# A mixture-of-experts layer: bias through the matrix product, one clamp, all weight slots split, the second product by column halves

## What is computed

```python
logits = (xt @ w_router) + b_router;  top_vals, top_idx = lax.top_k(logits, 4);  gates = softmax(top_vals)
# for each expert e and the tokens routed to it:
h = xblk @ w1[e] + b1[e]                      # 1024 x 2048
x_glu = minimum(h[..., ::2], 7);  x_lin = clip(h[..., 1::2], -7, 7)
a = x_glu * sigmoid(1.702 * x_glu) * (x_lin + 1)
out[token] += gate * (a @ w2[e] + b2[e])      # w2: 1024 x 1024
```

## Time and profile before

| | us |
|---|---|
| median of three runs | 2392.95 |
| the profiled execution | 2390.75 |
| its span, first to last instruction | 2389.0 |
| TensorE busy | 2191.3 (92%) |
| VectorE busy | 1499.4 (63%) |
| ScalarE busy | 972.6 (41%) |
| mean granted TensorE clock | 0.955 |

### The profile page before, as it was taken

How to read it: one execution, slowest core, us unless ns; L and a number is a source line. 1 busy time by engine, 2 the same in 40 slices (tenths; PEclk the granted TensorE clock), 3 DMA queues, 4 the chain that set the end, 5 groups by cost and what they waited for, 6 DMA issues and landing times.

```text
span 2389.0 us, 30180 instructions
## 1 busy us (share of the span) xinstructions
PE 2191.3 (92%) x9492; PEld 1592.8 (67%) x9493; DVE 1499.4 (63%) x2207; ACT 972.6 (41%) x1146; POOL 283.6 (12%) x245
## 2 busy tenths in 40 slices
PE   6999687997789999999899999999899999999997
PEld 4454277544468876686686868686667886886885
DVE  4013566233677676767777667777777677677765
ACT  3023444011344444444444444444444444444443
POOL 1000300001101111111011111111012012011111
PEclk9999799898799999999999999999999999999998
DMA  7000200200697669869978786868989668668666
GB/s 244 0 1 4 94 1 1 88 27 31 231 367 275 227 243 357 314 224 331 354 269 294 245 318 220 306 221 315 336 317 338 215 238 309 228 217 304 232 216 231
DMA packets 244997, 524.29 MB, mean 219 GB/s; under 512 B 17575, under 2 KB 22759, under 8 KB 240736
## 3 DMA queue, kind: packets, MB, share of 16 engines
q1 hardware_dynamic: 220990, 467.84, 54.8%
q0 software_dynamic: 23904, 55.95, 6.3%
q10 hardware_dynamic: 66, 0.02, 0.0%
HBM read 522.20 MB, written 32.11 MB: 232 GB/s over the span
## 4 chain that ended last, share of the span: by engine, by line
PE 76%; issue 4%; DVE 1%; DVEq 1%; ACT 1%; POOL 0%; POOLq 0%; ACTq 0%
PE ps L1028 19%; PE ps L1030 19%; PE ps L1029 19%; PE ps L1080 8%; PE ps L953 5%; PE ps L1063 2%; PE ps L1022 1%; PE ps L972 1%; PE ps L1015 1%; PE ps L985 1%; PE ps L965 0%; PE ps L934 0%; ACT uT L666 0%; DVE xT_lo L1469 0%; PE ps L907 0%
## 5 line engine op out<-in xcount | busy, mean ns | idle before, releaser
L1469 DVE TENSOR_TENSOR w_lo<-ring,w_hi 128x2048 fp32r<-128x2048 f32 x330 | 755.0, 2288 | 261.5 <-ACT w_hi L710 261.1
L710 ACT ACTIVATE w_hi<-ring 128x2048 fp32r<-128x2048 f32 x327 | 625.1, 1916 | 452.9 <-PE ps L1030 421.8
L1028 PE MATMUL ps<-w_hi,xT_hi 128*128 128x512 f32 x1212 | 499.5, 412 | 11.6 <-DVE xT_lo L1469 10.2
L1030 PE MATMUL ps<-w_hi,xT_lo 128*128 128x512 f32 x1212 | 474.9, 392 | 0.0
L1029 PE MATMUL ps<-w_lo,xT_hi 128*128 128x512 f32 x1212 | 473.3, 391 | 0.0
L1028 PE MATMUL ps<-w_hi,actT_hi 128*128 128x512 f32 x720 | 303.8, 422 | 73.7 <-issue 73.7
L1029 PE MATMUL ps<-w_lo,actT_hi 128*128 128x512 f32 x720 | 294.7, 409 | 0.0
L1030 PE MATMUL ps<-w_hi,actT_lo 128*128 128x512 f32 x720 | 294.0, 408 | 0.0
L1028 PEld LDWEIGHTS ps<-w_hi,xT_hi 128*128 128x128 f32 x1212 | 228.2, 188 | 76.4 <-issue 18.0
L1029 PEld LDWEIGHTS ps<-w_lo,xT_hi 128*128 128x128 f32 x1212 | 228.5, 188 | 53.2 <-issue 9.1
L1030 PEld LDWEIGHTS ps<-w_hi,xT_lo 128*128 128x128 f32 x1212 | 228.0, 188 | 50.2
(11 more groups left out here) (260 smaller groups left out, 2087.4 us busy)
## 6 DMA issues: line engine op xcount, KB each, us to landing
ring<-in_w SPq DMA_DIRECT2D x390, 1024.0 KB
b1b<-in_b SPq DMA_DIRECT2D x33, 1024.0 KB, 11.7
xh<-in_x SPq DMA_DIRECT2D x2, 2048.0 KB, 17.7
work<-in_w_out SPq DMA_DIRECT2D x1, 4096.0 KB, 12.7
token_rows<-uT POOLq DMA_DIRECT2D x8, 512.0 KB, 2.9
out<-xh SPq DMA_DIRECT2D x8, 512.0 KB, 2.6
work<-in_w_in SPq DMA_DIRECT2D x2, 1536.0 KB, 19.4
uT<-in_w_mem_kv SPq DMA_DIRECT2D x1, 2048.0 KB, 17.8
```

The costliest lines, as they stand in the source:

```text
L710: act_e.activation(w_hi[s % SPLIT][:, :, :], slot(s), ACT.Copy).then_inc(hi_ready, counted(s, whole))
L1028: pe.matmul(acc, hi, whi, start=first, stop=False)
L1030: return pe.matmul(acc, lo, whi, start=False, stop=last)
L1469: return dve.tensor_tensor(lo, x, hi.bitcast(F32), ALU.subtract)
```

## The change

- `add_bias` goes. The biases of all experts are put into SBUF once before the loop, as a high and a low part with 1 added in the odd columns (`b1w`). `select_expert` makes a 64 x 128 selection matrix for the pass on VectorE, and every odd slot begins with one matmul of it by 512 columns of `b1w`, for each group.
- VectorE then takes one minimum against a pair of limits, from PSUM (`clamp`); the lower clamp goes into `times_gelu`.
- ScalarE does `gelu(j)` ahead of `split_hi(2j+5)`, where it did it behind.
- No slot is left whole: single passes split all twelve.
- A slot of w2 now holds 256 rows by all 1,024 columns; `down(s, b)` computes one column half. Double passes run the halves b=0 of slots 8 and 9 and then the halves b=1. In single passes the results stand in banks 1 and 4 and the next tokens in 5 and 6, so the wait of slot 9 for `xlo_ready` is left to double passes; there it stands before `down(8, 1)`.
- `combine` moves from VectorE to ScalarE, as a copy out of PSUM times the gate, at the end of its list. The scatter adds into the output; the gather of the output rows is dropped. The 1 MB bias load of each pass is dropped.

```diff
+        def y_bank(groups, g, b):
+            return 4 * b + g if len(groups) == 2 else 1 + 3 * b
...
                     for g in groups:
-                        po.indirect_dma_start(out=rows[:, g, :], out_offset=None, in_=out[0],
...
                         po.wait_ge(combined[g], before[g] * 2 + 4)
+                        po.indirect_dma_start(out=out[0], out_offset=by_index(idx_cur, g), in_=y[:, g, :],
+                                              in_offset=None, bounds_check=last_row, oob_is_err=False,
+                                              compute_op=ALU.add).then_inc(scattered[g], 16)
...
+                    def combine(b):
+                        if b == 0:
+                            act_e.wait_ge(idxcur_ready, p + 1)
+                            act_e.wait_ge(gate_copied, p + 1)
+                            act_e.wait_ge(y_half, p + 1)
+                        else:
+                            act_e.wait_ge(w_used, p12 + (SPLIT + 12))
+                        for g in groups:
+                            act_e.activation(y[:, g, b * HALF:(b + 1) * HALF], ps[:, y_bank(groups, g, b), :], ACT.Copy,
+                                             scale=gate_cur[:, g:g + 1]).then_inc(combined[g], 1)
...
                     for j in range(4):
+                        gelu(j)
                         split_hi(2*j+5)
-                        gelu(j)
...
                     split_hi(13)
                     split_hi(14)
+                    combine(0)
+                    combine(1)
...
                         acc = ps[:, 2 * (j % 2) + g, :]
+                        if kh == 1:
+                            if j == 0:
+                                pe.wait_ge(b1_lo, 1)
+                                pe.wait_ge(sel_ready, p + 1)
+                            pe.matmul(acc, sel[:, :], b1w[:, j * HALF:(j + 1) * HALF], start=False, stop=False)
...
-                            if s in whole:
-                                m = pe.matmul(acc, xT_f[:, k, :], slot(s)[:, k, :], start=kk == 0, stop=kk == KD - 1)
...
+                    def down(s, b):
+                        j = s - 8
+                        if b == 0:
+                            wait_words(s)
                         for g in groups:
+                            if b == 0:
+                                pe.wait_ge(alo_ready[g], pieces[g] + (j + 1))
...
+                            for k in range(2):
+                                m = three(ps[:, y_bank(groups, g, b), :], actT_hi[g][:, 2 * j + k, :],
...
+                    down(8, 0)
+                    if len(groups) == 2:
+                        down(9, 0)
+                        transpose_act(2)
+                        pe.wait_ge(xlo_ready[0], p + 2)
+                        down(8, 1)
+                        down(9, 1)
+                    else:
+                        down(8, 1)
+                        transpose_act(2)
+                        down(9, 0)
+                        down(9, 1)
                     transpose_act(3)
+                    for s in (10, 11):
+                        down(s, 0)
+                        down(s, 1)
...
+                    def clamp(j):
+
+                        dve.wait_ge(w_used, used + (2 * j + 2))
                         for g in groups:
...
+                            dve.tensor_tensor(hm[:, g, j % 2, :], ps[:, 2 * (j % 2) + g, :],
+                                              limit[:, :, :].rearrange("p n two -> p (n two)"), ALU.min).then_inc(h_free[g], 1)
...
+                    select_expert()
                     split_lo(3)
...
+                    take_gates()
                     split_lo(4)
                     for j in range(4):
-                        add_bias(j)
+                        clamp(j)
...
-                        split_lo(2 * j + 5)
+                        if j < 3:
+                            split_lo(2 * j + 5)
+                        times_gelu(j)
                         if j == 3:
...
+                            split_lo(11)
                         if j:
                             take_alo(j - 1)
                         split_lo(2 * j + 6)
...
                     take_alo(3)
+                    if len(groups) == 1:
+                        take_xlo(p + 2, 0, next_x_bank(groups))
                     split_lo(13)
-                    combine(0)
                     split_lo(14)
-                    combine(1)
```

More of the change, by code:

```diff
@@ L178, in hymba_layer @@
         gatesT, b2_sb = uT[:, 11, :], uT[:, 12, :]
+        b1_raw = uT[0:2 * E, 0:2, :].rearrange("p a b -> p (a b)")
         early.close()
@@ L192, in hymba_layer @@
         actT_hi, actT_lo = ([sb(f"{n}{g}", [P, KD, P], F32R) for g in range(2)] for n in ("actT_hi", "actT_lo"))
[L193 to L196, removed]
+        sel = sb("sel", [2 * E, P], F32R)
+        hm = sb("hm", [P, 2, 2, HALF])
+        gel, act = (sb(n, [P, 2, 2, HALF // 2]) for n in ("gel", "act"))
+        y = sb("y", [P, 2, D])
         ps = ctx.enter_context(nc.psum_tensor("ps", [P, 8, HALF], F32))
@@ L275, in hymba_layer, with next_x_bank, ids_bank @@
             ptac.append(ptac[-1] + (heads(kind) // 2 + 1) // 2)
[L277 to L283, removed]
+        def next_x_bank(groups):
+            return 5 if len(groups) == 1 else 4
+        def ids_bank(groups):
+            return 3 if len(groups) == 1 else 6
+        def y_bank(groups, g, b):
+            return 4 * b + g if len(groups) == 2 else 1 + 3 * b
         def slot(s):
@@ L354, in _ @@
             sp.dma_start(b2_sb[0:E, :], b2[0]).then_inc(b2_in, 16)
+            for half in range(2):
+                sp.dma_start(b1_raw[half * E:(half + 1) * E, :], b1[0]).then_inc(b1_in, 16)
             sp.wait_ge(ttab_ready, 1)
@@ L1084, in up @@
[L1084 to L1104 removed]
+                            m = three(acc, xT_hi[g][:, kk, :], xT_lo[g][:, kk, :],
+                                      w_hi[s % SPLIT][:, k, :], w_lo[s % SPLIT][:, k, :], kk == 0, kk == KD - 1)
@@ L1483, in _ @@
             make_onehot(0)
-            make_idx(1)
+            make_idx(1, 6)
             make_onehot(1)
+            dve.wait_ge(b1_in, 32)
+            odd = b1_raw.rearrange("p (n two) -> p two n", two=2)[:, 1, :]
+            dve.tensor_scalar(odd, odd, 1.0, None, ALU.add).then_inc(b1_plus, 1)
             for u in range(2 * NT):
@@ L1556, in take_alo, with select_expert @@
                                      actT_hi[g][:, 2 * j:2 * j + 2, :]).then_inc(alo_ready[g], 1)
-                    def combine(b):
-                        dve.wait_ge(w_used, used + (11 + b))
-                        for g in groups:
-                            if b == 0:
-                                dve.wait_ge(rows_in[g], rows16[g])
-                            rb = rows[:, g, b * HALF:(b + 1) * HALF]
-                            dve.scalar_tensor_tensor(out=rb, in0=ps[:, 4 * b + g, :], scalar=gate_cur[:, g:g + 1], in1=rb,
-                                                     op0=ALU.mult, op1=ALU.add).then_inc(combined[g], 1)
+                    def select_expert():
+                        dve.tensor_tensor(sel[:, :], ident[0:2 * E, bass.ds(e, 1)].to_broadcast([2 * E, P]),
+                                          ident[0:2 * E, bass.ds(e + E, 1)].to_broadcast([2 * E, P]), ALU.add).then_inc(sel_ready, 1)
@@ L1579, in body @@
                         if j == 3:
-                            take_xlo(p + 2, 0)
-                        times_gelu(j)
+                            if len(groups) == 2:
+                                take_xlo(p + 2, 0, next_x_bank(groups))
+                            split_lo(11)
                         if j:
```

194 lines of the change are left out of this document (71 added, 123 removed).

## The result

The changed kernel takes 2552.4 us (2549.8 to 2553.4, four runs) against 2394.2 for the kernel before, measured beside it on the same chip: a ratio of 1.068 [1.066, 1.070]. It is slower, as forecast, but by 158 us instead of 87, and outside the range of the prediction. The profiled execution has a span of 2551.7 us.

The account below looks back on a forecast made before the run. VectorE's list with forced waits was taken to bound single passes after the change, TensorE double ones. 2390.75 + 57 (single) + 29 (double) + 1 (bias preparation) = 2478 us, slower; range 2440 to 2540 us.

Parts of the forecast that it names:

- Clamp to split_lo: VectorE in single passes: from clamp(j) it must wait for ScalarE's gelu, then split_hi; 3.0 us, four times, 12.0 us.
- TensorE's longest stop: Single passes: TensorE stands 4.9 us before activation transposes 3, waiting for take_alo(2), with 0.42 us matmul steps behind.
- the sign that was to speak for the scatter: If VectorE's longest stop came before the index step, the scatter would be the cause; no size given.
- It gets eight bias matmuls: 1.8 us: Double passes: TensorE stays the bound and pays 1.8 us for eight added bias matmuls.
- 0.4 us more of stop at the head: Head of double passes: TensorE waits for the second group's low part, between 0 and 0.65 us, taken as 0.4.
- the same duration is hidden, with 0.6 in hand: Single passes: 7.81 us from scatter issue to index copy still fits before VectorE's gap closes, 0.6 us to spare.
- no longer than a plain one: The adding scatter was taken to last as long as a plain one; the alternative was 3.8 us more.
- Rival 3: Adding scatter late: moving part twice as long, 3.2 us more per single pass, 61 us in all, 2539 us; chance 0.10.
- 3.0 for each: Single passes: each of the 19 gets 3.0 us longer, 57 us in all; a steady one takes 46.4 us.
- rival 1: TensorE's clock does not fall, or falls where it costs nothing: 30 us less, 2448 us; chance 0.18.
- Rival 2: TensorE's clock stays low through slots 10 and 11 of single passes: 72 us more, 2550 us; chance 0.10.
- Rival 4: Faster: VectorE's gaps do not add up and TensorE sets single passes at 36.2 + 0.5 us, total 2286 us; chance 0.07.

Follow-up runs that it names:

- run 1: The changed kernel with ScalarE's split_hi(2j+5) put back ahead of gelu(j), nothing else: 2421.4 us, 1.013 of the kernel before.
- run 4: The changed kernel with a plain scatter that overwrites rows instead of the adding one, sum over experts left out: 2536.1 us, 1.061 of the kernel before.
- run 2: The changed kernel with selection matrix and bias rows padded from 64 to 128 partitions: 2519.3 us, 1.054 of the kernel before.
- run 3: The changed kernel without the bias products, first-layer bias left out, selection matrix still made: 2495.1 us, 1.044 of the kernel before.
- run 5: The changed kernel with VectorE's index step moved from behind clamp(0) to behind times_gelu(0): 2541.8 us, 1.065 of the kernel before.
- run 6: The changed kernel with split_hi ahead of gelu, the index step behind times_gelu(0) and the bias product at 128 rows: 2349.4 us, 0.984 of the kernel before.

## Why the prediction was right and wrong

**Right: the mechanism and the side.** Clamp to split_lo was put at 3.0 us; it is 3.00 (1870.76 - 1867.76). The clamps were forecast 7.7, 9.7 and 8.1 us apart, and are 8.5, 9.6 and 8.1 apart. TensorE's longest stop is before activation transposes 3, with 0.43 us steps behind, the stop before slot 9 is gone, and VectorE's 2.3 us waits before split_lo(7) and split_lo(9) end with ScalarE's w_hi. Run 1 undoes this one cause and gives back 131 us.

Some of the signs did not come as written. The passes are 47.8 and 75.2 us, not 46 to 47 and 72 to 73. Before split_lo(5) the wait is for the index copy, and at 2.83 us it is VectorE's longest in the steady pass, the sign that was to speak for the scatter; runs 1 and 4 show that the order weighs 131 us and the adding scatter 16. TensorE's stop is 3.06 us and not 4.9: a second slow stretch of six steps behind activation transposes 2, which the forecast did not have, fills 1.2 us of it.

**Wrong: three sizes.**
- *The bias product, "It gets eight bias matmuls: 1.8 us".* The step that failed is to take a matmul of 64 rows at the price of one of 128, 0.227 us. Runs 2 and 3 show 4.19 us for the eight, and 0.63 for one by itself: (4.19 - 1.8) x 13 = 31 us too little. The other term, 0.4 us more of stop at the head, comes out near: without the products the stretch is 0.5 us longer than before, and the stop 1.15 us where it was 0.62 (run 3). Forecast 29 for the double passes, measured 61.
- *The adding scatter, "the same duration is hidden, with 0.6 in hand".* For a plain scatter that holds (run 4): VectorE's wait of 1.49 us lies inside the 2.3 us gap. The step that failed is "no longer than a plain one": issue and landing together are 1.3 us longer, which is over the 0.6, and it costs 16 us. Rival 3 named the mechanism at 61 us. The moving part is not twice as long, and it is the passes behind a double one that have no slack for it. The sentence cited there from the Trainium skill, that an engine takes turns between its queues, spoke against this rival; the index copy still comes 8.35 us after the issue of a transfer of one group's rows, and the runs don't tell whether that is turns or transfer.
- *The single pass, "3.0 for each".* Taking the scatter's 16 from the 92 us leaves 76, which is 4.0 each, 19 us too little. In the steady pass, 47.8 where 46.4 was forecast, 0.8 of it is the wait for the index copy at clamp(0) (8.5 instead of 7.7) and 0.7 the turn of the loop: clamp(3) to clamp(0) took 21.6 where 20.9 was forecast, with ScalarE's first split_hi late, so that VectorE waits 1.39 us before one split_lo of the second pass. But runs 4 and 5 show that such terms don't simply add up: the first of them was made smaller, and the pass stayed. So this split of the 1.4 us into two causes is argued, not shown.

In the two profiled executions 162.7 us were lost where 87 was forecast. Of the 76 missed, 32 are in the double passes, 31 of them the price of the product, and 35 in the single ones (16 and 19). The other 8 lie outside the stretches compared, 9 where 1 was forecast. Of these, the 4.8 us before the loop are no steady cost: the same part took 0.8 us more in runs 2 and 4.

**Rivals.** The clock did fall, eight steps behind the long stop as forecast, against rival 1. Rival 2 gave 2550, almost the measured time, for another reason: slots 10 and 11 do return to the short step (1885.72), and the second slow stretch lies ahead of the long stop, where it only shortens it. The time alone would have spoken for the wrong rival. Rival 4, that the gaps don't add up, is refuted by the result and by run 1. Yet the number that it used is instructive: TensorE alone was put at 36.2 us for a single pass, and run 6, in which nothing forces VectorE to stand behind a clamp, has 36.7 busy and passes of 39.1 to 41.0. The change had a good part that its order on ScalarE hid.

**Range.** It ended at 2540, 12 us short. I had let the unknown costs vary one at a time. All three went the same way, and none of the bounds of a matmul with fewer rows or of the scatter was added to the others. The price of the product alone, 31 us, would have brought the measured time inside.

## What to carry to other kernels

When two engines in order hand work to each other, write down for each wait what is queued behind it: a short gelu in front of a split that the other engine wants next cost 131 us here, and exchanging two lines gave it back. Before believing that a change is bad, take its parts one by one: with the order, the index step and the bias product repaired this one beats the kernel before by 38 us. Splitting all slots has no part in that; by itself it cost 50 us in the kernel before, and in the repaired kernel leaving three slots unsplit is as fast. And an operand that is only smaller may not be cheaper: pad it and measure.

## What the runs showed of the hardware

- A product with 64 rows in the stationary operand among such with 128 cost 0.63 us, with 128 rows 0.23 (steps at 770.71 and 768.02): its own weight load and the next one began with their matmuls and not one matmul early.
- An adding indirect scatter took 1.6 us of GpSimd's issue where a plain one took 1.02 at the same place, 1.3 us more from issue to the dependent copy, and 16 us over 45 of them.
- The clock answers for more than the stops: the same matmuls took TensorE 39.9 us at a granted clock of 0.93 (run 2) and 36.7 at 1.00 (run 6). Of the 8.7 us between the steady passes of the changed kernel and run 6 (47.8 - 39.1), 4.0 are idle time (6.4 - 2.4), 3.2 the slower clock and 1.5 the four products of 64 rows.
- Steady single passes of mostly 47.7 to 48.0 us in five kernels with different terms inside (the changed one, runs 3, 4 and 5, and the kernel before with the order alone): two chains of nearly equal length are seen, the equality itself is not explained.
